# Reordering the units, the work ahead of the first unit and the slot fill in a mixture-of-experts layer whose weights stream from memory

## Chip, cores and metric

One core of one Trainium2 chip runs the whole program. The metric is device time in microseconds (us) of one execution, the median over several. The chip's parts are named as in the profile: PE is TensorE, DVE is VectorE, ACT is ScalarE, POOL is GpSimd, SP is SyncE, which here only issues transfers.

## The reference, cut to what matters

Two trunk layers over 384 tokens (128 context, 256 latent) of width 1024. In each layer a mixer (convolution, Hyena and attention groups) is followed by a mixture of 64 experts, of which each token takes 8, and by one shared expert that takes all tokens. Only the mixture is touched:

```python
def swiglu(x, wg, wu, wd):
    return (jax.nn.silu(x @ wg) * (x @ wu)) @ wd

def moe(h, p):
    s = jax.nn.sigmoid(h @ p['router_w'])
    # 4 of 8 groups by their two best (s + bias), then the 8 best experts in them
    w = w / jnp.sum(w, axis=-1, keepdims=True) * ROUTED_SCALE
    # every expert runs on the tokens that chose it; results are weighted and summed per token
    y_buf = lax.map(expert_block, (x_buf, block_e))
    routed = jax.ops.segment_sum(y_buf * w_buf[:, None], tok_buf, ...)
    return swiglu(h, p['sh_w_gate'], p['sh_w_up'], p['sh_w_down']) + routed
```

An expert has three fp32 matrices, gate and up (1024 x 256 each) and down (256 x 1024): 1 MiB each, 3 MiB an expert, 192 MiB for the 64 experts of a layer. All are read in each layer.

## The kernel before, in words

**Units.** The experts are sorted by their number of tokens and get fixed numbers of slots: 11 experts of 96 slots are paired with 11 of 32, 38 of 64 slots are paired among themselves, and 4 get 128 slots alone. So there are 34 units of 128 slots: 30 pair units (numbers 0 to 29; 0 to 10 are 96 and 32) and 4 full units (30 to 33). `parts` gives a unit's slots, `WIDE` the order in which the units run, `JOBS` the experts n = 1 to 64 in that order, `OWNER` the step that uses n. Before, the order begins with the full units 30 and 31, then pairs 0 to 5, full unit 32, pairs 11 to 17, full unit 33, and the other pairs.

**Buffers and SP.** Four weight buffers of 3 MiB (two in RING, two in WB) take the experts in turn: expert n goes to buffer n % 4. The shared expert is n = 0 and lies in buffer 0, which is next wanted by expert 4. SP issues the loads in program order from one queue (L517 and L518 the gate and up matrices, L522 the down matrix): for each step first gate and up of its experts, then their down matrices. `free` makes gate and up of n wait until the gate and up product of the step that owns n - 4 is done, and the down matrix until that step's down products are done; for n = 4 it waits for `sh_gu` and `sh_dn`, the last use of the shared expert's matrices for the third token tile. The stream starts when DVE has the order of the experts (`d_ord`, L1726). In layer 0 SP also loads the next layer's parameters after step 2.

**Ahead of the first unit, on PE (`mixture_pe`).** An order written out by hand mixes the routing's products (counts, order, positions: L1063 to L1086) with the shared expert's work for token tiles 1 and 2: `shared_up` (gate and up, 8 slices of k), `shared_flip` (transposes of the activation, L966), `shared_down` (two halves of columns, L959), two calls of `gate_rows` (L824, which lay the layer's output gate out as rows for ACT's `grow`), and `lists` for units 0 to 2 (L977, L980: which token sits in which slot). `lists` and `shared_flip` share PSUM bank 7.

**On DVE (`mixture_dve`).** After the positions are in place (`place`, from L1731), `onehot` builds a unit's slot matrix (L1766), `list_out` copies the list out of PSUM (L1776), `lst` turns it into gather indices (L1784: 16 small operations, four for each quarter g of the slots) and weights, `shared` makes the shared activation, and `turned` transposes the gathered rows of a unit (L1831).

**On POOL (`mixture_pool`).** `gather` issues four indirect DMAs a unit (L564). Issue g fetches the rows of slots 32g to 32g + 31, each in four parts of 1 KB: partition 32r + i takes part r of the row of slot 32g + i. Indices of empty slots are out of bounds, and their rows aren't moved. A unit's filled slots are, in each expert's range, the first ones. `scat` builds the matrix that sends a unit's outputs back to tokens (L572).

**A step (`step`, on PE).** Gate and up products of the unit (L946, 8 slices of k, both experts of a pair in parallel column groups), lists of unit s + 3, scatter of unit s - 1 (L993, L994), transposes (L966), down products (L959). Step 0 has the second half of the shared down product of tile 2 in place of the scatter.

## Time and profile before

| | |
|---|---|
| median of 3 runs | 1730.71 us (1730.41 to 1733.8) |
| the profiled execution | 1731.37 us, span 1729.5 us |
| PE busy | 1583.1 us (92%) |
| DVE, ACT, POOL busy | 840.1, 346.4, 425.5 us |
| DMA | 530.59 MB, mean 307 GB/s |
| experts' loads, first layer | first issued at 315.3 us of the span |
| experts' loads, second layer | first issued at 1163.6 us |

A window's row gives, behind the window and its length, the busy time of PE, of its weight loads (PEld), DVE, ACT and POOL with the number of instructions in brackets, then the granted TensorE clock (1.00 is 2.4 GHz, 0.50 is 1.2 GHz), the mean busy share of the 16 DMA engines (it shows 1.01 to 1.02 where all are busy) and the GB/s moved. A timeline row gives the start, the duration, engine, line, operation, output and inputs, and in square brackets the idle time before it with what ended it. Matmuls overlap, so a group of PE rows lasts a few tenths less than shown where another follows at once.

### The profile page before, as it was taken

Reading aid. Unit: us, or ns where it says so; the run is one execution under the profiler, and the core shown is the slowest. Engines: PE = TensorE matmul, PEld = TensorE weight load, DVE = VectorE, ACT = ScalarE, POOL = GpSimd, SP = SyncE. Lnnn points to the kernel's source line nnn. Section 1 sums busy time; section 2 is a strip of 40 time slices with the busy share of each in tenths; the row PEclk is TensorE's granted clock in tenths of the full one; section 3 lists DMA queues with packets and bytes.
Section 4 is the critical chain, followed back from the end, with each engine's and each line's share of the span. In section 5 each row is a group of like instructions: output and inputs, shape, how many; then the busy total and the mean of one; then the engine's idle time right before and its main releaser. Section 6 shows DMA issues by size and latency. Waiting matters only on the chain.

```text
span 1729.5 us, 22727 instructions
## 1 busy us (share of the span) xinstructions
PE 1583.1 (92%) x7900; PEld 791.3 (46%) x7900; DVE 840.1 (49%) x2813; ACT 346.4 (20%) x776; POOL 425.5 (25%) x421
## 2 busy tenths in 40 slices
PE   6999899899998998888979997998999899889886
PEld 2865355544443434434347553554444344344333
DVE  3777553644443443444165856455444434343332
ACT  2501443111111111111152014431111111111111
POOL 0300010143332332333013000004333323332320
PEclk9999999999999999999989999999999999999998
DMA  9322825779999999999632239028999999999993
GB/s 398 142 104 98 345 105 195 292 290 413 413 413 413 413 412 412 413 413 414 285 128 98 104 104 395 1 82 333 369 412 412 416 413 412 412 414 413 413 415 141
DMA packets 80851, 530.59 MB, mean 307 GB/s; under 512 B 13968, under 2 KB 17308, under 8 KB 25184
## 3 DMA queue, kind: packets, MB, share of 16 engines
q1 hardware_dynamic: 67680, 503.90, 71.9%
q0 software_dynamic: 13056, 25.22, 4.0%
q8 instruction: 64, 1.05, 0.2%
q14 instruction: 51, 0.42, 0.1%
HBM read 533.76 MB, written 5.77 MB: 312 GB/s over the span
## 4 chain that ended last, share of the span: by engine, by line
PE 58%; DMA 31%; DVE 6%; issue 2%; SPq 2%; ACT 1%; POOL 0%; DVEq 0%; ACTq 0%
PE PSB L946 21%; DMA WB<-in_exp_w_up 21%; DMA RING<-in_exp_w_up 8%; PE PSB L938 7%; PE PSB L959 6%; PE PSB L874 4%; PE PSB L993 2%; PE PSB L994 2%; PE PSB L689 2%; PE PSB L910 1%; PE PSB L920 1%; PE PSB L911 1%; PE PSB L933 1%; SPq L517 1%; PE PSB L732 1%
## 5 line engine op out<-in xcount | busy, mean ns | idle before, releaser
L946 PE MATMUL PSB<-RING,EX 128*32 128x512 f32 (+2 forms) x1344 | 409.1, 608 | 44.9 <-DMA WB<-in_exp_w_up 31.1
L946 PE MATMUL PSB<-WB,EX 128*32 128x512 f32 (+2 forms) x1408 | 417.8, 600 | 30.1 <-DMA RING<-in_exp_w_up 23.3
L564 POOL DMA_INDIRECT XG<-h_rows,IDX x272 | 279.0, 1026 | 181.2 <-issue 94.4
L959 PE MATMUL PSB<-RING,AT 128*32 128x512 f32 (+2 forms) x720 | 227.0, 598 | 4.8 <-ACT GROW L1298 3.7
L572 POOL TENSOR_SCALAR SCAT<-CST,LSTT 128x384 fp32r<-128x384 f32 x68 | 84.9, 1248 | 561.3 <-PE PSB L994 561.1
L946 PEld LDWEIGHTS PSB<-WB,EX 128*32 128x32 f32 (+2 forms) x1408 | 128.2, 127 | 191.1 <-issue 191.1
L946 PEld LDWEIGHTS PSB<-RING,EX 128*32 128x32 f32 (+2 forms) x1344 | 123.2, 128 | 199.0 <-issue 199.0
L959 PE MATMUL PSB<-WB,AT 128*32 128x512 f32 (+2 forms) x704 | 210.8, 596 | 0.0
L1852 DVE TENSOR_TENSOR YL<-PSB,YH 128x512 fp32r<-128x512 f32 x136 | 94.0, 691 | 186.0 <-ACT YH L1378 186.0
L1776 DVE COPY LCOL<-PSB 128x6 f32<-128x6 f32 x68 | 11.2, 164 | 345.8 <-PE PSB L977 312.8
L993 PE MATMUL PSB<-YH,SCAT 128*128 128x512 f32 x408 | 171.8, 421 | 2.8 <-DVE YL L1852 2.8
L1784 DVE TENSOR_SCALAR IDX<-LCOL 32x1 int32<-32x1 f32 x1088 | 157.3, 145 | 31.9
L994 PE MATMUL PSB<-YL,SCAT 128*128 128x512 f32 x408 | 161.0, 395 | 0.0
L1371 ACT ACTIVATE SGM<-PSB 128x256 f32<-128x256 f32 x68 | 26.1, 383 | 531.6 <-PE PSB L946 531.6
L1378 ACT ACTIVATE YH<-PSB 128x512 fp32r<-128x512 f32 x136 | 81.2, 597 | 239.6 <-PE PSB L959 239.6
L938 PE MATMUL PSB<-RING,HT 128*128 128x512 f32 x288 | 125.9, 592 | 0.0
L556 POOL TENSOR_TENSOR ST<-ST,HALF 128x1 f32<-128x1 f32 x48 | 28.6, 595 | 301.4 <-DVE ST L2150 133.8
L959 PEld LDWEIGHTS PSB<-RING,AT 128*32 128x32 f32 (+2 forms) x720 | 62.8, 129 | 79.1 <-issue 75.2
L959 PEld LDWEIGHTS PSB<-WB,AT 128*32 128x32 f32 (+2 forms) x704 | 58.4, 126 | 72.4 <-issue 71.9
L993 PEld LDWEIGHTS PSB<-YH,SCAT 128*128 128x128 f32 x408 | 77.6, 190 | 21.2 <-issue 4.9
L1831 DVE STREAM_TRANSPOSE EX<-XG 128x1024 f32<-128x1024 f32 x68 | 84.2, 1238 | 6.4 <-DMA XG<-h_rows,IDX 6.3
L874 PE MATMUL PSB<-RING,YT 128*128 128x512 f32 x192 | 85.7, 593 | 0.0
(287 smaller groups left out, 1832.5 us busy)
## 6 DMA issues: line engine op xcount, KB each, us to landing
RING<-in_exp_w_gate SPq DMA_DIRECT2D x64, 1024.0 KB
RING<-in_exp_w_up SPq DMA_DIRECT2D x64, 1024.0 KB
RING<-in_exp_w_down SPq DMA_DIRECT2D x64, 1024.0 KB, 20.6
WB<-in_exp_w_gate SPq DMA_DIRECT2D x64, 1024.0 KB, 16.6
WB<-in_exp_w_up SPq DMA_DIRECT2D x64, 1024.0 KB, 20.6
WB<-in_exp_w_down SPq DMA_DIRECT2D x64, 1024.0 KB, 20.7
RING<-in_wmod SPq DMA_DIRECT2D x16, 2048.0 KB, 11.2
KSYS<-in_wmod SPq DMA_DIRECT2D x8, 2048.0 KB, 10.5
```

Source lines behind the costliest of these rows:

```text
L564: pool.indirect_dma_start(XG[:, s % 2, g * 256:(g + 1) * 256], None, h_quarters, bass.IndirectOffsetOnAxis(ap=IDX[:, s, g:g + 1], axis=0), ...
L572: nc.gpsimd.tensor_scalar(SCAT[:, s % 2, :], cst("iota"), LSTT[:, s:s + 1], None, ALU.is_equal).then_inc(p_scat, 1)
L874: mm = nc.tensor.matmul(PS[YB[0][t] + hf][:, :], YT[:, f, t * P:(t + 1) * P], w[:, f, :], start=(f == 0), stop=(f == 7))
L938: mm = nc.tensor.matmul(PS[3 + i % 3][:, :], HT[:, k, t * P:(t + 1) * P], w[:, k, :], start=(k == 0), stop=(k == KD - 1))
L946: mm = nc.tensor.matmul(PS[6][s0:s0 + w, :].rearrange("p (w f) -> p w f", w=2), e(k, s0, w), rawgu[n % NBUF][:, k], start=(k == 0), stop=( ...
L959: mm = nc.tensor.matmul(dst[s0:s0 + w, :], AT[:, j, s0:s0 + w], rawdn[n % NBUF][:, hf, j], start=(j == 0), stop=(j == 1))
L993: nc.tensor.matmul(PS[piece][:, :], w, YHb[s % 2][:, cols], start=False, stop=False, skip_group_check=True)
L994: mm = nc.tensor.matmul(PS[piece][:, :], w, YLb[s % 2][:, cols], start=False, stop=True, skip_group_check=True)
L1378: sc.activation(YHb[s % 2][:, hf * 512:(hf + 1) * 512], PS[6 + hf][:, :], ACT.Copy).then_inc(a_yh, 1)
L1784: v.tensor_scalar(IDX[32 * r:32 * r + 32, s, g:g + 1], LCOL[32 * g:32 * g + 32, 4:5], 4.0, 4.0 * NONE + r, ALU.mult, ALU.add).then_inc(d_l ...
L1831: v.transpose(EX2[:, s % 2].rearrange("p k (g j) -> p g k j", g=4), XG[:, s % 2, :].rearrange("p (g k j) -> p g k j", g=4, k=KD)).then_inc ...
L1852: v.tensor_tensor(YLb[s % 2][:, hf * 512:(hf + 1) * 512], PS[6 + hf][:, :], YHb[s % 2][:, hf * 512:(hf + 1) * 512].bitcast(F32), ALU.subtr ...
```

## The change

It has these parts:

- **Unit order.** `WIDE` begins with the pair units 0 to 5, 11, 12; the full units come at steps 8, 15, 22 and 29.
- **SP order.** The down matrix of expert 4 (now the second expert of step 1) is issued behind gate and up of step 2's experts.
- **PE order.** Both `gate_rows` move ahead of the position products, the shared gate and up slices move behind them, `lists` of unit 0 comes ahead of the last slices, and `lists` of unit 2 and the shared down products of tiles 1 and 2 move into step 0. Tile 2 has its own buffer AT2 for the transposed activation. ACT's and DVE's orders follow.
- **Gather waits.** Each of a unit's four gathers waits for its own four indices, not for the whole list.
- **DVE order.** The transpose of unit 0's rows comes ahead of unit 1's index operations, and that of unit 1 at the end of step 0's activation.
- **Slot fill.** In steps s >= 3 with s odd the slot matrix compares with reversed ranks (IOTAR), so that the filled slots are the last ones of each expert's range. IOTAR costs one DVE operation a layer.

```diff
@@ -162,7 +162,9 @@
             YL1 = sb("YL1", [P, DM], F32R, c=me)
-            sb("unused1", [P, (NT - 2) * DM], c=me)
+            AT2 = sb("AT2", [P, 2, P], c=me)
+            IOTAR = sb("IOTAR", [P, P], c=me)
+            sb("unused1", [P, (NT - 2) * DM - 3 * P], c=me)
@@ -272,7 +274,8 @@
-        WIDE = (30, 31) + tuple(range(0, 6)) + (32,) + tuple(range(11, 18)) + (33,) + tuple(range(6, 11)) + tuple(range(18, 30))
+        WIDE = (tuple(range(0, 6)) + (11, 12, 30) + tuple(range(13, 18)) + (6, 31) + tuple(range(7, 11)) + (18, 19, 32)
+                + tuple(range(20, 26)) + (33,) + tuple(range(26, 30)))
@@ -509,6 +512,7 @@
                 sp.wait_ge(d_ord, l + 1)
+                late = []
                 for s, job in enumerate(JOBS):
@@ -516,10 +520,15 @@
-                    for (n, c, cap, tiles), e in zip(job, es):
+                    for (n, c, cap, tiles), e in late + list(zip(job, es)):
                         b = n % NBUF
+                        if n == NBUF and s == OWNER[n]:
+                            late = [((n, c, cap, tiles), e)]
+                            continue
                         free(l, n, True)
                         sp.dma_start(raw[b][:, 4096:6144], row(I["exp_w_down"], l, e)).then_inc(dn_in[b], 16)
+                    if s > OWNER[NBUF]:
+                        late = []
@@ -557,16 +566,17 @@
             def gather(l, s):
-                pool.wait_ge(d_lst, LSTN * (NU * l + s + 1))
                 if s >= 2:
                     pool.wait_ge(d_ex, NU * l + s - 1)
                 for g in range(4):
+                    pool.wait_ge(d_lst, LSTN * (NU * l + s) + 4 * (g + 1))
                     pool.indirect_dma_start(XG[:, s % 2, g * 256:(g + 1) * 256], None, h_quarters,
...
             def scat(l, s):
+                pool.wait_ge(d_lst, LSTN * (NU * l + s + 1))
                 if s >= 2:
@@ -821,7 +831,7 @@
-                    mm = nc.tensor.matmul(PS[(2, 4)[r] + k // 4][:, (k % 4) * P:(k % 4 + 1) * P],
+                    mm = nc.tensor.matmul(PS[2 + k // 4][:, (k % 4) * P:(k % 4 + 1) * P],
@@ -951,12 +961,12 @@
-            def down(job, hf, dst):
+            def down(job, hf, dst, a=AT):
...
@@ -1006,14 +1016,22 @@
                 for k in range(KD):
                     mm = gate_up(job, slots(s % 2), k)
+                    if s == 0 and k == 3:
+                        pe.wait_ge(sh_ah, NT * l + 3)
+                        lists(l, 2)
                 mm.then_inc(pe_gu, 1)
                 if s > 0:
                     pe.wait_ge(d_yl, 2 * (NU * l + s))
+                else:
+                    pe.wait_ge(d_lcol, NU * l + 3)
                 if s + 3 < NU:
                     lists(l, s + 3)
                 if s > 0:
                     scatter(l, s - 1, (0, 1, 2, 3))
                 else:
+                    shared_down(l, 1, 0)
+                    shared_down(l, 1, 1)
+                    shared_down(l, 2, 0)
                     shared_down(l, 2, 1)
@@ -1046,10 +1064,10 @@
-                if t == 2 and hf == 0:
+                if t == 1 and hf == 0:
                     pe.wait_ge(a_grow, 8 * (l + 1))
                 pe.wait_ge(sh_ah, NT * l + t + 1)
-                mm = down(SHARED, hf, PS[2 * t + hf])
+                mm = down(SHARED, hf, PS[2 * t + hf], AT2 if t == 2 else AT)
@@ -1057,7 +1075,7 @@
                 shared_flip(l, 0)
-                shared_up(l, 1, 0, 3)
+                gate_rows(l, 1, 0)
                 pe.wait_ge(d_cnt, l + 1)
@@ -1074,36 +1092,31 @@
                 mm.then_inc(pe_ord, 1)
-                shared_up(l, 1, 3, 6)
+                shared_up(l, 1, 0, 2)
                 pe.wait_ge(d_sw, l + 1)
...
-                shared_up(l, 1, 6)
+                gate_rows(l, 1, 1)
                 pe.wait_ge(a_stk, l + 1)
...
                 mm.then_inc(pe_perm, 1)
+                shared_up(l, 1, 2, 6)
+                pe.wait_ge(sh_ah, NT * l + 1)
+                lists(l, 0)
+                shared_up(l, 1, 6)
                 shared_down(l, 0, 0)
                 shared_down(l, 0, 1)
-                lists(l, 0)
                 pe.wait_ge(d_lcol, NU * l + 1)
                 shared_flip(l, 1)
-                shared_up(l, 2)
-                pe.wait_ge(d_sort, SORTN * (l + 1))
-                gate_rows(l, 1, 0)
-                shared_down(l, 1, 0)
-                shared_down(l, 1, 1)
-                pe.wait_ge(d_lcol, NU * l + 1)
+                shared_up(l, 2, 0, 3)
+                pe.wait_ge(sh_ah, NT * l + 2)
                 lists(l, 1)
+                shared_up(l, 2, 3)
                 pe.wait_ge(d_lcol, NU * l + 2)
                 shared_flip(l, 2)
-                gate_rows(l, 1, 1)
-                pe.wait_ge(sh_ah, NT * l + 3)
-                lists(l, 2)
-                shared_down(l, 2, 0)
-                pe.wait_ge(d_lcol, NU * l + 3)
                 for s in range(NU):
@@ -1353,19 +1366,22 @@
             def mixture_act(l):
                 shared_turned(l, 0)
-                shared_sig(l, 1)
+                grow(l, 1, 0)
                 act.wait_ge(pe_sw, l + 1)
                 sc.activation(STK[:, :, :].rearrange("p t s -> p (t s)"), PS[5][:, 0:NT * P], ACT.Copy).then_inc(a_stk, 1)
+                grow(l, 1, 1)
+                shared_sig(l, 1)
                 shared_turned(l, 1)
                 shared_sig(l, 2)
-                grow(l, 1, 0)
                 shared_turned(l, 2)
-                grow(l, 1, 1)
@@ -1763,7 +1779,8 @@
-                    ins = v.tensor_tensor(ONEHOT[:, s % 2, :, s0:s0 + cap], cst("iota")[:, 0:cap].unsqueeze(1).to_broadcast([P, NT, cap]),
+                    ranks = IOTAR[:, P - cap:P] if s >= 3 and s % 2 == 1 else cst("iota")[:, 0:cap]
+                    ins = v.tensor_tensor(ONEHOT[:, s % 2, :, s0:s0 + cap], ranks.unsqueeze(1).to_broadcast([P, NT, cap]),
@@ -1812,16 +1829,14 @@
                 onehot(l, 0)
-                shared(l, 1)
+                onehot(l, 1)
                 list_out(l, 0)
                 lst(l, 0)
-                onehot(l, 1)
-                shared(l, 2)
-                onehot(l, 2)
+                shared(l, 1)
                 list_out(l, 1)
-                lst(l, 1)
-                list_out(l, 2)
-                lst(l, 2)
+
+                dve.wait_ge(h_out, 16 * NT * (l + 1))
+                do(v.tensor_scalar(IOTAR[:, :], cst("iota")[:, 0:P], -1.0, float(P - 1), ALU.mult, ALU.add), d_rt)
@@ -1832,10 +1847,15 @@
                 turned(0)
+                lst(l, 1)
+                shared(l, 2)
+                onehot(l, 2)
+                list_out(l, 2)
+                lst(l, 2)
                 for s in range(NU):
                     if s + 3 < NU:
                         onehot(l, s + 3)
-                    if s + 1 < NU:
+                    if 1 <= s < NU - 1:
                         turned(s + 1)
@@ -1847,6 +1867,8 @@
                     if s + 3 < NU:
                         lst(l, s + 3)
+                    if s == 0:
+                        turned(1)
```

## Rows read from the trace of the kernel before

**Rows 1.** Profile page: the gathers' DMA queue (packets, MB, share) and the chain by engine.
```profile
q0 software_dynamic: 13056, 25.22, 4.0%
...
PE 58%; DMA 31%; DVE 6%; issue 2%; SPq 2%; ACT 1%; POOL 0%; DVEq 0%; ACTq 0%
```

**Rows 2.** Windows: start:end, length, busy by engine, granted clock, DMA share, GB/s.
```profile
318.00:344.00 26.00, 22.71 (x89) 12.83 (x87) 13.71 (x78) 5.94 (x9) 6.62 (x7) 0.97 1.01 419
344.00:384.00 40.00, 38.73 (x153) 18.08 (x152) 19.62 (x74) 4.31 (x9) 17.74 (x17) 0.93 0.73 278
384.00:840.00 456.00, 418.97 (x2356) 186.78 (x2357) 193.74 (x774) 58.44 (x119) 156.37 (x146) 0.99 1.01 413
1194.00:1232.00 38.00, 37.44 (x163) 17.91 (x165) 19.42 (x81) 4.69 (x10) 16.89 (x17) 1.00 0.71 267
```

**Rows 3.** Chain that ended last, end of the first layer's loads: start, us, what.
```profile
814.32 24.39 DMA WB<-in_exp_w_up
838.80 9.83 PE PSB L946 x32
```

**Rows 4.** The same chain, a pair unit and full unit 32: start, us, what.
```profile
445.91 7.07 PE PSB L946 x64
...
460.11 7.07 PE PSB L946 x16
```

**Rows 5.** Timeline of the SP queue, first layer: start, us, instruction.
```profile
315.29 0.37 SPq L517 DMA_DIRECT2D RING<-in_exp_w_gate  x1
...
331.75 0.34 SPq L517 DMA_DIRECT2D RING<-in_exp_w_gate  x1
...
356.49 0.33 SPq L522 DMA_DIRECT2D RING<-in_exp_w_down  x1
```

**Rows 6.** Timeline of PE, first layer, 313 to 355.
```profile
313.60 2.79 PE L946 MATMUL PSB<-RING,HT 128*128 128x512 f32 x6
...
319.29 0.94 PE L1086 MATMUL PSB<-PERM,STK 128*128 128x128 f32 x6 [0.85 <-ACT STK L1363]
320.06 3.60 PE L959 MATMUL PSB<-RING,AT 128*128 128x512 f32 x8
...
324.52 7.03 PE L946 MATMUL PSB<-RING,HT 128*128 128x512 f32 x16
331.39 1.95 PE L824 MATMUL PSB<-CST,GC 128*128 128x128 f32 x16
...
345.21 9.20 PE L946 MATMUL PSB<-RING,EX 128*128 128x512 f32 x16 [0.71 <-DVE EX L1831]
```

**Rows 7.** Timeline of PE, second layer, the same gate and up product.
```profile
1193.59 7.11 PE L946 MATMUL PSB<-RING,EX 128*128 128x512 f32 x16 [1.59 <-DVE EX L1831]
```

**Rows 8.** Timeline of DVE, first layer.
```profile
322.71 0.56 DVE L1766 TENSOR_TENSOR ONEHOT<-CST,POSS 128x384 fp32r<-128x384 f32 x1
...
324.16 2.78 DVE L1784 TENSOR_SCALAR IDX<-LCOL 32x1 int32<-32x1 f32 x16
...
343.82 1.25 DVE L1831 STREAM_TRANSPOSE EX<-XG 128x1024 f32<-128x1024 f32 x1
```

**Rows 9.** Timeline of POOL, first layer.
```profile
328.20 1.27 POOL L564 DMA_INDIRECT XG<-h_rows,IDX  x1 [30.81 <-DVE LSTW L1790]
...
332.38 1.00 POOL L564 DMA_INDIRECT XG<-h_rows,IDX  x1 [0.30 <-issue]
```

**Rows 10.** Tile XG, 400 to 840: time of the gathers from issue to landing.
```profile
DMA to landing us min/median/max: 5.8/6.3/7.8
```

**Rows 11.** Windows at the end of each layer's loads: columns as in Rows 2.
```profile
845.00:858.00 13.00, 13.00 (x62) 5.75 (x60) 2.29 (x4) 1.96 (x4) 1.24 (x1) 1.00 0.47 196
1690.00:1703.00 13.00, 13.00 (x62) 5.71 (x60) 2.29 (x4) 1.96 (x4) 1.24 (x1) 1.00 0.54 226
```

**Rows 12.** Short windows inside the first of these.
```profile
846.00:848.00 2.00, 2.00 (x12) 0.65 (x10) 0.00 (x0) 0.00 (x0) 0.00 (x0) 1.00 0.83 340
...
854.00:856.00 2.00, 2.00 (x12) 0.66 (x10) 0.69 (x1) 0.88 (x2) 0.00 (x0) 1.00 0.24 98
```

More of the change, by code:

```diff
@@ L958, in down @@
                         for s0, w in tiles:
-                            mm = nc.tensor.matmul(dst[s0:s0 + w, :], AT[:, j, s0:s0 + w], rawdn[n % NBUF][:, hf, j],
+                            mm = nc.tensor.matmul(dst[s0:s0 + w, :], a[:, j, s0:s0 + w], rawdn[n % NBUF][:, hf, j],
                                                   start=(j == 0), stop=(j == 1))
@@ L1298, in grow @@
                     own.sig(sc.activation(g[:, cond, 4 * b:4 * b + 4, :],
-                                          PS[(2, 4)[r] + b][:, :].rearrange("t (k q) -> t k q", k=4), ACT.Copy), a_grow)
+                                          PS[2 + b][:, :].rearrange("t (k q) -> t k q", k=4), ACT.Copy), a_grow)
             def squares(l, r, t):
@@ L1355, in shared_turned @@
                 act.wait_ge(sh_at, NT * l + t + 1)
-                sc.activation(AT[:, :, :].rearrange("p j s -> p (j s)"), PS[7][:, 0:DE], ACT.Copy).then_inc(sh_ah, 1)
+                if t == 2:
+                    act.wait_ge(h_out, 16 * NT * (l + 1))
+                a = AT2 if t == 2 else AT
+                sc.activation(a[:, :, :].rearrange("p j s -> p (j s)"), PS[7][:, 0:DE], ACT.Copy).then_inc(sh_ah, 1)
             def mixture_act(l):
                 shared_turned(l, 0)
-                shared_sig(l, 1)
+                grow(l, 1, 0)
                 act.wait_ge(pe_sw, l + 1)
                 sc.activation(STK[:, :, :].rearrange("p t s -> p (t s)"), PS[5][:, 0:NT * P], ACT.Copy).then_inc(a_stk, 1)
+                grow(l, 1, 1)
+                shared_sig(l, 1)
                 shared_turned(l, 1)
                 shared_sig(l, 2)
-                grow(l, 1, 0)
                 shared_turned(l, 2)
-                grow(l, 1, 1)
                 for s in range(NU):
```

## The prediction

> **What bounds the kernel now.** I read the page first: PE is busy 92% of the span, yet the chain that ended last has 31% DMA in it [rows 1]. The windows say where. From 384 to 840, nearly the whole first mixture, all 16 DMA engines are busy (share 1.01 at 413 GB/s), and PE is busy 419 of 456 us [rows 2]; just before, from 344 to 384, the share is 0.73, and in the second layer 0.71 for 38 us, with PE at work nearly throughout. So a layer's mixture is a stream of weights that nothing in it shortens, with a hole of 40 x (1 - 0.73/1.01) = 11.1 us near its start in the first layer and 38 x (1 - 0.71/1.01) = 11.3 us in the second. At the other end the chain goes from a load that lands at 838.7 straight to the product that waited for it [rows 3], and from there PE alone sets the end: whatever makes the stream's last loads land earlier shortens the layer one for one. Faster PE work inside the stream is worth nothing.
>
> **Why there is a hole.** The chain shows a pair unit's gate and up products taking 7.07 us, and those of full unit 32 also 7.07 us [rows 4]: a pair's experts run side by side. Between these two starts lie 14.2 us, a whole step. A pair brings 6 MiB in that time, which at 413 GB/s is 15.2 us of stream; a full unit brings 3 MiB, 7.6 us. With full units first, PE spends two steps on freeing what feeds the stream for 15 us. In the SP queue [rows 5] the loads start at 315.29, expert 4's gate matrix is issued at 331.75 and its down matrix only at 356.49, after the shared expert's last down product; SP issues in order, so everything else stands behind it. By then 11 MiB and two units' gathers are issued: a unit's gathers are 25.22 MB / 68 = 0.37 MB [rows 1]. That is 12.3 MB, or 29.3 us at the 419 GB/s of this stretch [rows 2], and the stream runs dry at 345.6.
>
> **The change at the start, step by step (first layer).** The start of the stream is fixed by the expert order, whose products end ahead of 313.60 [rows 6]; ahead of them two gate_rows (the first only) replace three slices, and a row of gate_rows (1.95) is shorter than what it replaces, 3/8 of 7.03 [rows 6]. I cost that at nothing. From 313.60: two slices 1.75 (2/8 of 7.03), three transposes of SW (0.4, by half of the six in L1086's 0.94), the second gate_rows 1.8 as it overlaps, so the position products start at 317.5 where they started at 319.29 [rows 6]: they no longer wait for ACT's STK, which stood behind a sigmoid. DVE's slot matrix follows 3.4 us behind, at 320.9 and not 322.71; those of units 0 and 1 end at 322.2, as one for a pair costs about what the full one's 0.56 does [rows 8]. PE's four slices last until 321.9, the list until 322.5; DVE's 16 index operations (2.78) begin at 322.7, and the first four are done at 323.4 [rows 8]. Before, POOL's first gather began at 328.20, 1.0 after the whole list was done; now it waits for four indices, begins at 324.4, and the fourth, 4.2 us behind the first as before, at 328.6 instead of 332.38 [rows 9]. The median from issue to landing is 6.3 [rows 10], so unit 0's rows are there at 334.9, and the transpose (1.25, [rows 8]) ends at 336.1. Before, the transpose waited until 343.82 behind DVE's index work.
>
> DVE has a new order, and that is where the change waits: the transpose stands ahead of unit 1's indices (2.78, and 0.3 for its three small operations), and the shared activation of tile 2 (two operations a little smaller than a slot matrix's 0.56, 0.9) behind them. It ends at 340.1. PE, with 1.75 + 3.6 + 0.4 + 2.65 + 0.7 + 4.4 = 13.5 us of slices, down products and list behind 322.5, is through at 336.0 and idles 4 us. Then a transpose of 0.4, and the first product starts at 340.5 and not 345.21. With unit 2's list in its middle it takes 7.1 + 0.5, to 348.1. The 0.4, 0.5 and 0.7 are estimates from 0.94 for six small products [rows 6].
>
> SP: expert 4's gate can go when tile 2's slices end, at 336.0 and not 331.75. The stream has 8 MiB and one unit's gathers, 8.8 MB or 20.9 us from about 316.3, until 337.2; with the 1.3 that I take from issue to data it just meets it. No row isolates that time: its bounds are 0 and the fastest gather's 5.8 [rows 10], and I stay near the lower, since SP's loads need no indices fetched; each layer's hole moves one for one with it, before as after, so it cancels in the difference but for this meeting. Its down matrix no longer blocks: it goes behind experts 5 and 6, whose gates wait only for step 0's product at 348.1. Hence the hole runs from 345.6 to 349.4, **3.8 us**. Next are 4 MiB (10.2 us), to 359.6; expert 4's down matrix is free after four shared down halves of 1.8 [rows 6], 348.7 + 7.1 = 355.8, in time. Step 0's down products end at 360.8 and free 2 MiB; step 1 then frees gate buffers at 367.9, when the stream has work to 367.7 (in the first layer the parameters' 1 MiB more). I allow 0.2 in the first layer and 1.2 in the second. Holes of 4.0 and 5.0 stand against 11.1 and 11.3: **gain 7.1 + 6.3 = 13.4 us**. POOL's gathers for unit 1 end issuing near 341.7 and land near 348, its transpose is wanted only at 360.8; the matrices of `scat` keep their place. In later steps a full unit takes PE 14 us against 8.5 of stream, a deficit of 5.5, a pair 14 against 16.1: six pairs between two full units bring 12 and cover it. I cost the four late full units at nothing; without the cover each costs up to 5.5 us.
>
> **Slot fill.** At the ends of the streams the busy share doesn't fall at once: 845 to 858 it is 0.47, 1690 to 1703 it is 0.54 [rows 11]. Against the mean engine, the last one ends (1 - 0.47/1.01) x 13 = 7.0 us late in the first layer and 6.1 in the second. The weights are equal rows for all; the gathers move 0.37 MB where full slots would be 0.52 (4 x 128 x 1 KB), and the empty ones are always each range's last. Bounds: 0, if an engine's share doesn't hang on the slot, and 7.0 + 6.1. The fall is gradual (0.83 at 846, 0.24 at 854, [rows 12]), as a sloping share of gather work over the engines would give, so I take the upper end less a tenth for steps 0 to 2, filled forward, and chance: **gain 6.3 + 5.4 = 11.7 us**. The Trainium skill's DMA: Bandwidth & Descriptors, The descriptor swizzle, gives the engine of a 128-partition transfer by its group of four partitions, modulo eight within each half; with this gather's index layout that is the slot's group of four modulo eight, which reversed ranks mirror. By it the gain would be near 12. No row here names an engine.
>
> **Sum.** 1731.4 - 13.4 - 11.7 = 1706.3 for the profiled execution, which lies 0.7 above the median: **1706** rounded. The reversed-ranks operation, less than a slot matrix's 0.56, is hidden in DVE's wait for rows.
>
> **Rivals.**
> - *The slope isn't from the slots.* Then 13.4 alone: 1718. For it: no row shows which engine carries what. Against it: the gradual fall. Chance 0.15. The skill's same page, Latency and other measured facts, says engines 7 and 15 are usually slower; two late engines of 16 would leave a share near 0.12 throughout, and the levels of 0.83 and 0.24 here speak against that rule.
> - *The first product gains nothing*, since PE's 4 us idle brings the clock to 1.2 GHz or DVE is later. Half clock cost 9.20 against 7.11 [rows 6, 7], 2.1 a layer; the whole loss is 13.4: 1719. Chance 0.12.
> - *It doesn't do what it says*: neither hole nor slope moves, 1730. Chance 0.04.
> - *Slower: unit 0's rows come late.* DVE's transpose now blocks unit 1's indices and tile 2's activation, and PE and SP stand behind that. Each us of later landing makes the hole a us longer. It takes 14 us a layer, 20 from issue to landing instead of 6.3, to be slower by 0.2%; at 22, 1706 + 2 x 16 = 1738. The slowest gather took 7.8 [rows 10]. Chance 0.03.
> - *More is gained*: no hole at all, 9.0, 1697. Chance 0.08.
>
> **The numbers.** The forecast has 0.58. The range takes in the two part-gains above and most of the best case: 1698 to 1719. Apart by 0.2% (3.5 us) is about what a measurement of this kernel can tell. Faster: 0.58 + 0.15 + 0.12 + 0.08 = 0.93; same 0.04; slower 0.03.
>
> **What would show it.** In the new profile: position products at 317.5, first gather 324.4, first unit's product at 340.5; expert 4's down matrix issued behind those of experts 5 and 6's gates; a hole of about 4 us from 345.6; the share at the stream's end falling from 1.0 to 0 within 3 us; full units' steps with PE waiting no less in the pairs around them. A hole of 10 us, a tail as long as before, or DMA share under 1.0 around steps 15, 22 and 29 would prove me wrong.

## The result, and the profile after

The changed kernel takes **1715.26 us** (median of 4 executions, 1713.72 to 1716.95) where the kernel before takes 1731.14 beside it (1730.41 to 1733.8): a ratio of 0.9896 with a 95% interval of 0.9879 to 0.9914, some 16 to 18 us less. Run again later it took 1715.84, ratio 0.9897 (0.9879 to 0.9915). So it is faster, within the range of 1698 to 1719, but 9 us above the 1706 of the forecast: of 25.1 us expected, about two thirds came. Two executions of this study, one of the kernel before (2312.13 us, mean granted clock 0.657) and one of a variant below (2709.96 us, 0.556), ran at a far lower clock than the 0.97 to 0.98 of all others and are left out of the ratios.

The page of the changed kernel: the first rows and the chain by engine, which answer to [rows 1].

```profile
span 1714.6 us, 22803 instructions
...
PE 1583.5 (92%) x7900; PEld 792.1 (46%) x7900; DVE 841.0 (49%) x2815; ACT 347.2 (20%) x776; POOL 426.2 (25%) x421
...
DMA packets 80852, 530.60 MB, mean 309 GB/s; under 512 B 13968, under 2 KB 17308, under 8 KB 25184
...
PE 62%; DMA 26%; DVE 6%; issue 2%; ACT 1%; SPq 1%; POOL 0%; DVEq 0%; ACTq 0%
```

Work and bytes are the same as before (the gathers' queue too, 25.22 MB); what changed is waiting. The chain has 26% DMA in it and not 31%.

Windows of the same kernel: the start of each layer's stream, its middle and its end, to be laid beside [rows 2, 11].

```profile
344.00:384.00 40.00, 38.68 (x282) 15.11 (x285) 19.67 (x84) 4.31 (x9) 17.39 (x17) 0.97 0.93 371
384.00:840.00 456.00, 429.74 (x2280) 194.02 (x2273) 195.95 (x780) 59.31 (x121) 156.85 (x146) 0.99 1.02 413
838.00:851.00 13.00, 12.03 (x56) 5.34 (x54) 2.29 (x4) 1.96 (x4) 1.24 (x1) 1.00 0.58 241
847.00:849.00 2.00, 2.00 (x12) 0.86 (x10) 0.01 (x1) 0.00 (x0) 0.00 (x0) 1.00 0.12 49
1188.00:1226.00 38.00, 36.75 (x269) 14.45 (x265) 19.59 (x84) 3.93 (x8) 14.87 (x14) 0.98 0.84 336
1676.00:1689.00 13.00, 12.05 (x56) 5.37 (x54) 2.29 (x4) 1.97 (x4) 1.24 (x1) 1.00 0.64 267
1686.00:1688.00 2.00, 2.00 (x12) 0.86 (x10) 0.00 (x0) 0.00 (x0) 0.00 (x0) 1.00 0.07 29
```

Read with the prediction's method. The holes are (1 - 0.93/1.02) x 40 = 3.5 us and (1 - 0.84/1.02) x 38 = 6.7 us; before they were 11.1 and 11.3. (Run again, the changed kernel had shares of 0.93 and 0.90 in the same windows: 3.5 and 4.5 us.) The middle is saturated as before, at the same 413 GB/s, with all four full units in it, so the late full units cost nothing. At the ends, whose windows here stop with the last load (851.0 and 1689.1), the mean engine is (1 - 0.58/1.02) x 13 = 5.6 and (1 - 0.64/1.02) x 13 = 4.8 us ahead of the last; before it was 7.0 and 6.1. So the start gave 7.6 + 4.6 = 12.2 us, nearly the 13.4 forecast, and the ends 1.4 + 1.3 = 2.7 where 11.7 was forecast. Together that is 14.9 of the 16 to 18 us measured.

The chain at the end of the first layer's loads, which answers to [rows 3] (start, us, what):

```profile
825.68 20.84 DMA RING<-in_exp_w_up
...
846.61 7.09 PE PSB L956 x32
```

Still a load that lands last and a product that waited for it, now for the last unit. Before, the load at 838.7 was that of the last unit but one. PE then worked without a wait, and the chain of the kernel before has the last unit's product as

```profile
855.44 6.88 PE PSB L946 x32
```

with nothing of DMA ahead of it. So before, the chain left the DMA engines 6 us ahead of the window in which the busy share falls (845 to 858), and what lands last, the down matrices at 858.0, wasn't wanted until 865.5. The prediction had counted the whole lateness in that window as time of the layer. Nor is the product behind the wait the same: it took 9.83 us, with the granted clock at 0.55 from 838 to 845, and takes 7.09 in the changed kernel.

Timelines of the changed kernel around the first unit, first layer: SP, POOL, DVE, PE. A row has start, us, engine, line, operation, output and inputs, and the idle time before it.

```profile
318.79 0.37 SPq L521 DMA_DIRECT2D RING<-in_exp_w_gate  x1
...
352.98 0.34 SPq L521 DMA_DIRECT2D RING<-in_exp_w_gate  x1
...
361.00 4.79 SPq L529 DMA_DIRECT2D RING<-in_exp_w_down  x2
...
326.82 1.27 POOL L573 DMA_INDIRECT XG<-h_rows,IDX  x1 [26.47 <-DVE IDX L1801]
...
331.01 1.00 POOL L573 DMA_INDIRECT XG<-h_rows,IDX  x1 [0.30 <-issue]
...
338.06 1.25 DVE L1846 STREAM_TRANSPOSE EX<-XG 128x1024 f32<-128x1024 f32 x1 [4.53 <-DMA XG<-h_rows,IDX]
339.23 2.75 DVE L1801 TENSOR_SCALAR IDX<-LCOL 32x1 int32<-32x1 f32 x16
...
342.89 0.42 DVE L1815 TENSOR_TENSOR ACTV<-PSB,ACTV 128x256 f32<-128x256 f32 x1
...
320.42 0.83 PE L1104 MATMUL PSB<-PERM,STK 128*128 128x128 f32 x6
...
333.06 4.54 PE L956 MATMUL PSB<-RING,HT 128*128 128x512 f32 x10
343.46 0.67 PE L976 MATMUL PSB<-CST,ACTV 128*128 128x128 f32 x2 [5.86 <-DVE ACTV L1815]
344.06 1.08 PE L956 MATMUL PSB<-RING,EX 128*32 128x512 f32 x3
```

DVE stands idle for 4.53 us waiting for unit 0's rows, then does the transpose, unit 1's indices and tile 2's activation one after the other, and PE waits 5.86 us for the last of them. That is the wait the prediction named, only longer.

### The profile page after: what moved, and what is told of

It is laid out like the page before. It is cut to its first block, busy times and chain, and to the rows that moved or that the text cites. A ratio compares the mean times of both kernels' runs of the same rounds, so it can differ in the third digit from the quotient of the medians.

```text
span 1714.6 us, 22803 instructions
## 1 busy us (share of the span) xinstructions
PE 1583.5 (92%) x7900; PEld 792.1 (46%) x7900; DVE 841.0 (49%) x2815; ACT 347.2 (20%) x776; POOL 426.2 (25%) x421
## 3 DMA queue, kind: packets, MB, share of 16 engines
q0 software_dynamic: 13056, 25.22, 4.0%
## 4 chain that ended last, share of the span: by engine, by line
PE 62%; DMA 26%; DVE 6%; issue 2%; ACT 1%; SPq 1%; POOL 0%; DVEq 0%; ACTq 0%
PE PSB L956 22%; DMA RING<-in_exp_w_up 16%; DMA WB<-in_exp_w_up 8%; PE PSB L969 7%; PE PSB L948 7%; PE PSB L884 4%; PE PSB L1003 3%; PE PSB L1004 3%; PE PSB L699 2%; PE PSB L943 1%; PE PSB L920 1%; PE PSB L930 1%; PE PSB L921 1%; PE PSB L742 1%; SPq L521 1%
## 5 line engine op out<-in xcount | busy, mean ns | idle before, releaser
L956 PE MATMUL PSB<-RING,EX 128*32 128x512 f32 (+2 forms) x1408 | 375.1, 610 | 28.7 <-DMA RING<-in_exp_w_up 14.8
L956 PE MATMUL PSB<-WB,EX 128*32 128x512 f32 (+2 forms) x1344 | 373.3, 600 | 23.9 <-DMA WB<-in_exp_w_up 12.9
L969 PE MATMUL PSB<-RING,AT 128*32 128x512 f32 (+2 forms) x752 | 210.5, 596 | 1.1 <-ACT AT L1389 1.1
L956 PEld LDWEIGHTS PSB<-RING,EX 128*32 128x32 f32 (+2 forms) x1408 | 115.8, 127 | 185.8 <-issue 185.8
L956 PEld LDWEIGHTS PSB<-WB,EX 128*32 128x32 f32 (+2 forms) x1344 | 115.8, 127 | 177.4 <-issue 177.4
L969 PE MATMUL PSB<-WB,AT 128*32 128x512 f32 (+2 forms) x672 | 189.1, 597 | 0.0
L969 PEld LDWEIGHTS PSB<-WB,AT 128*32 128x32 f32 (+2 forms) x672 | 51.9, 126 | 69.3 <-issue 68.9
## 6 DMA issues: line engine op xcount, KB each, us to landing
RING<-in_wmod SPq DMA_DIRECT2D x16, 2048.0 KB, 11.3
```

Source lines behind the costliest of these rows:

```text
L956: mm = nc.tensor.matmul(PS[6][s0:s0 + w, :].rearrange("p (w f) -> p w f", w=2), e(k, s0, w), rawgu[n % NBUF][:, k], start=(k == 0), stop=( ...
L969: mm = nc.tensor.matmul(dst[s0:s0 + w, :], a[:, j, s0:s0 + w], rawdn[n % NBUF][:, hf, j], start=(j == 0), stop=(j == 1))
```

## The experiments

All are edits of the kernel before, of the changed one, or of the version with indices first below; each shows the lines that matter. The text on record stands ahead of each measurement. Times are medians; "before" is the kernel before on the same chip, 1732.44 for the first four, 1733.75 for the next four and 1732.55 for the last four. The holes and latenesses are worked out from windows as above, by 1.01 or 1.02 as the middle of the stream shows it.

### The slot fill: four runs

**Fill alone.** The kernel before, with reversed ranks in odd steps from step 3 on, and nothing else:

```diff
+            IOTAR = sb("IOTAR", [P, P], c=me)
...
+                    ranks = IOTAR[:, P - cap:P] if s >= 3 and s % 2 == 1 else cst("iota")[:, 0:cap]
...
```

> The kernel before with the reversed fill in odd steps from 3 on and nothing else. In the trace of the changed kernel the last DMA engine ends 10.9 us (first layer) and 7.9 us (second) sooner after the first load than before, of which the shorter hole explains 8.0 and 4.9. Theory: the rest, 3.0 us a layer, is the slot fill's, so this kernel takes 1731 - 6 = 1725 us, and its busy share at the streams' ends falls within about 6 us instead of 12. As forecast (11.7 us for the fill): 1719 us. Rival (the fill does nothing, the rest has another cause): 1731 us and a fall over 12 us.

Measured: 1729.8 us (10 executions, 1726.45 to 1732.74), ratio 0.9985 (0.9971 to 1.0): 2.6 us, at most 5. The 11.7 of the forecast is far outside, and so is the theory's 6. Its windows at the ends of the streams and around the second layer's hole, and that last one for the kernel before:

```profile
843.00:856.00 13.00, 12.01 (x55) 5.45 (x55) 2.29 (x4) 1.97 (x4) 1.24 (x1) 1.00 0.67 279
1689.00:1702.00 13.00, 12.00 (x56) 5.43 (x54) 2.29 (x4) 1.97 (x4) 1.24 (x1) 1.00 0.72 297
1188.00:1232.00 44.00, 41.33 (x157) 19.23 (x158) 23.02 (x97) 5.55 (x12) 20.16 (x19) 0.92 0.68 262
```
```profile
1188.00:1232.00 44.00, 39.99 (x169) 18.95 (x172) 24.61 (x109) 6.65 (x12) 20.55 (x20) 1.00 0.75 287
```

The lateness falls from 7.0 and 6.1 to (1 - 0.67/1.01) x 13 = 4.4 and (1 - 0.72/1.01) x 13 = 3.7 us, 5.0 less in all and not 11.7: even with balanced slots more than half of it stays. And not all of the 5.0 shows in the time. In this profile the second layer's hole is (1 - 0.68/1.01) x 44 = 14.4 us where it was 11.3, with its first product at the lower clock (9.07 us and not the 7.11 of [rows 7]). Whether other executions lost time in the same way isn't known.

**Everything but the fill**, and **all units from the last slot on.** The changed kernel with one condition altered:

```diff
-                    ranks = IOTAR[:, P - cap:P] if s >= 3 and s % 2 == 1 else cst("iota")[:, 0:cap]
+                    ranks = IOTAR[:, P - cap:P] if False else cst("iota")[:, 0:cap]
```

> The changed kernel with every unit filled forward. Theory (the fill is worth 3.0 us a layer): 1715 + 6 = 1721 us, the share at the end falls over 12 us again, the holes near the start stay at about 3 and 6 us. As forecast (11.7): 1727 us. Rival (the fill does nothing): 1715 us.

```diff
+                    ranks = IOTAR[:, P - cap:P] if s >= 3 else cst("iota")[:, 0:cap]
```

> The changed kernel with all steps from 3 on filled from the last slot. If an engine's gather work hangs on the slot alone and the engines are otherwise equal, this is the mirror image of the forward fill: same time as that kernel, 1721 us by the theory, and a fall over 12 us. In the changed kernel one of 16 engines still ends 3 us behind the others in both layers (a share of 0.06 for 3 us). If it is one of those that the first slots load, the mirror image takes work from it: the share of 0.06 at the end goes, and the time is 1718 us. If it is one that the last slots load, its lateness adds to the load: 1724 us or more. Rival (the fill does nothing): 1715 us.

Measured: forward 1718.8 (1717.03 to 1722.01), ratio 0.9919 (0.9903 to 0.9936); all reversed 1719.41 (1716.81 to 1720.65), ratio 0.9923 (0.9906 to 0.994). Against 0.9896 of the alternating fill both are 4 to 5 us slower, and equal to each other; their intervals overlap that of the changed kernel at the edge.

The same windows at the ends of the streams, each stopping within 0.7 us of its last load: forward, then all reversed.

```profile
843.00:856.00 13.00, 12.05 (x56) 5.44 (x54) 2.29 (x4) 1.96 (x4) 1.24 (x1) 1.00 0.54 224
1682.00:1695.00 13.00, 12.03 (x56) 5.43 (x54) 2.29 (x4) 1.96 (x4) 1.24 (x1) 1.00 0.61 254
```
```profile
841.00:854.00 13.00, 12.07 (x56) 5.61 (x56) 2.29 (x4) 1.96 (x4) 1.24 (x1) 1.00 0.57 235
1680.00:1693.00 13.00, 12.06 (x56) 5.61 (x56) 2.29 (x4) 1.96 (x4) 1.24 (x1) 1.00 0.63 260
```

The shares hardly differ from the 0.58 and 0.64 of the changed kernel: here too most of the lateness at a stream's end is there with balanced slots. What follows: the slots do matter, since only the mixture of both directions gains and one direction is worth what the other is. But the fill is worth about 4 us in both layers together, and the fall at the end is a poor measure of it. On the kernel before it fell by 5.0 us for 2.6 of time; between these profiles it differs by 1 us at most for 4 of time, and forward fill under the changed start already ends a little less late (6.1 and 5.2) than before (7.0 and 6.1).

A fourth run settles the size on another base (the version with indices first, below), where no hole interferes:

```diff
-                    ranks = IOTAR[:, P - cap:P] if s >= 3 and s % 2 == 1 else cst("iota")[:, 0:cap]
+                    ranks = IOTAR[:, P - cap:P] if False else cst("iota")[:, 0:cap]
```

> The kernel with the index operations first and every unit filled forward. The fill was worth 0.23% of the time, some 4 us, on the changed kernel, and 0.15% on the kernel before. Theory (it works in the stream, whatever the start does): 4 to 5 us more than the kernel beside it, 1710 us, and the busy share at the stream's end falls over 9 us or more. Rival (part of it was given back in the holes): 7 us or more.

Measured: 1710.06 (1707.81 to 1711.28), ratio 0.9867 (0.9845 to 0.9889), against 1705.53, ratio 0.9843 (0.982 to 0.9866), of its base in the same session: 4.2 us by the ratios, 4.5 by the medians. That is the theory's 4 to 5, and not the rival's 7. The intervals overlap, but four comparisons by ratios (2.6 for the fill alone, 4.0 and 4.7 against forward and all reversed, 4.2 here) say the same.

### The DVE order ahead of the first unit

```diff
-                turned(0)
                 lst(l, 1)
                 shared(l, 2)
+                turned(0)
                 onehot(l, 2)
```

> The changed kernel with DVE's index operations of unit 1 and the shared activation of tile 2 ahead of the transpose of unit 0's rows. In the changed kernel DVE idles 4.5 us before that transpose and PE 5.9 us behind the work that comes after it. Theory (the hole that is left hangs on this order): the first unit's product starts 3.7 us sooner, the first layer's hole of 3 us goes, the second layer's of 6.4 us shrinks to about 3, and the time falls by 6 to 7 us to 1708 or 1709. Rival (what holds the stream is expert 4's gate, issued when tile 2's slices end): product sooner, hole and time as they are, 1715 us.

Measured: **1705.29** (1703.54 to 1710.61), ratio 0.9854 (0.9831 to 0.9877): 7 to 10 us faster than the changed kernel. Its timeline of PE and of SP, and two windows, one in each layer:

```profile
330.07 4.54 PE L956 MATMUL PSB<-RING,HT 128*128 128x512 f32 x10
336.09 0.48 PE L976 MATMUL PSB<-CST,ACTV 128*128 128x128 f32 x2 [1.49 <-DVE ACTV L1815]
337.24 0.63 PE L956 MATMUL PSB<-RING,EX 128*32 128x512 f32 x3 [0.67 <-DVE EX L1846]
...
345.09 0.34 SPq L521 DMA_DIRECT2D RING<-in_exp_w_gate  x1
...
344.00:384.00 40.00, 38.76 (x283) 16.73 (x275) 20.97 (x91) 4.92 (x11) 16.38 (x16) 1.00 1.02 412
...
1182.00:1222.00 40.00, 39.43 (x287) 16.97 (x290) 20.39 (x85) 5.20 (x11) 16.02 (x15) 1.00 1.01 404
```

DVE now does the index work and the activation while the rows are on their way, instead of behind them. PE waits 1.49 us and not 5.86, in this profile its clock is 1.00 throughout, and the next gates are issued 29.3 us after the first load (315.80), while by the prediction's account the stream has work until 30.3 after: the shares are 1.02 and 1.01, both holes are gone. The wait of 5.86 us was worth the whole remaining hole, and more than the 6 to 7 us expected. So the prediction's small rival "more is gained" was there to be had, one swap away.

The same kernel again, as the base for later runs:

> The changed kernel with unit 1's index operations and tile 2's activation ahead of unit 0's transpose, again, beside the kernels of this call. Ratio to the kernel before 0.985 as in the first call, 1705 to 1708 us, no hole in either layer.

Measured: 1705.53 (1702.53 to 1707.72), ratio 0.9843 (0.982 to 0.9866). PE waits the same 1.49 us in its profile, but here the clock does fall, to 0.74 from 338 to 342 and 0.84 from 342 to 346. The stream has no hole all the same (shares of 1.01 from 344 to 384 and 1.02 from 1174 to 1214).

### The parts of the start: order, down matrix, gather waits

**The changed kernel with the old unit order:**

```diff
+        WIDE = (30, 31) + tuple(range(0, 6)) + (32,) + tuple(range(11, 18)) + (33,) + tuple(range(6, 11)) + tuple(range(18, 30))
```

> The changed kernel with the unit order of the kernel before (full units 30 and 31 first), all else as changed. Theory (a full unit takes PE the 14 us of a step and frees only 3 MiB of the stream): holes of 11 us or more in each layer, in two or three pieces, and 1731 us, as before the change. Rival (the moved shared down products and the earlier gathers carry the gain, the order of the units nothing): 1715 us, holes of 3 and 6 us.

Measured: 1734.11 (10 executions, 1730.41 to 1736.13), ratio 0.9997 (0.9985 to 1.0009). Its SP timeline and its windows, one in each layer:

```profile
354.51 0.34 SPq L520 DMA_DIRECT2D RING<-in_exp_w_gate  x1
...
374.08 0.33 SPq L520 DMA_DIRECT2D WB<-in_exp_w_gate  x1
...
350.00:380.00 30.00, 28.65 (x82) 14.26 (x81) 17.02 (x80) 3.32 (x7) 11.83 (x11) 1.00 0.58 216
1198.00:1224.00 26.00, 24.72 (x69) 11.90 (x68) 14.15 (x62) 2.34 (x5) 9.49 (x9) 0.99 0.38 135
```

A full unit's product frees one expert's gate and up, and between two such releases (354.51 and 374.08) lies more than a step. The holes are (1 - 0.58/1.01) x 30 = 12.8 and (1 - 0.38/1.01) x 26 = 16.2 us. All other parts of the change together show no gain without the order.

**The kernel before with the new unit order alone:**

```diff
+        WIDE = (tuple(range(0, 6)) + (11, 12, 30) + tuple(range(13, 18)) + (6, 31) + tuple(range(7, 11)) + (18, 19, 32)
+                + tuple(range(20, 26)) + (33,) + tuple(range(26, 30)))
```

> The kernel before with the new unit order and nothing else. Theory (SP issues in order, and expert 4's down matrix waits for tile 2's down product at the end of step 0): one hole of about 10 us stays in each layer, the short ones behind it go, 1728 to 1730 us. Rival (the order alone carries the gain of the start): holes of 3 and 6 us, 1718 us.

Measured: 1726.71 (10 executions, 1724.73 to 1729.91), ratio 0.9973 (0.996 to 0.9986): 4.7 us by the ratio, 7.0 by the medians. The windows around its two holes:

```profile
350.00:361.00 11.00, 10.44 (x85) 4.10 (x81) 4.79 (x23) 0.77 (x2) 6.72 (x7) 1.00 0.38 120
1194.00:1205.00 11.00, 10.44 (x81) 3.75 (x85) 4.52 (x21) 0.77 (x2) 7.29 (x7) 0.99 0.40 113
```

Holes of 6.9 and 6.6 us are left of 11.1 and 11.3, 8.9 less, and 5 to 7 us of it show in the time. In the profiled executions the two mixtures, each from its first load to the last activation, take 11.6 us less than before, while the whole takes 5.3 less (1726.04 against 1731.37). The rest lies outside the mixtures: the first load comes at 319.83 and not 315.29, and 1.7 us more lie between the first mixture and the second.

**The changed kernel with expert 4's down matrix issued in its old place:**

```diff
-                        if n == NBUF and s == OWNER[n]:
+                        if False:
```

> The changed kernel with expert 4's down matrix issued in its own step, ahead of gate and up of experts 5 and 6. It waits for tile 2's down product, which now comes behind step 0's gate and up product. Theory (SP issues in order): gates 5 and 6 are issued 8 to 9 us later, each hole grows by as much, 1715 + 17 = 1732 us, as much as the whole change had gained. Rival (the stream has enough issued by then): 1715 us.

Measured: 1727.63 (median of 10; nine of them from 1725.8 to 1730.08), ratio 0.9971 (0.9957 to 0.9986): 12 to 13 us slower than the changed kernel where 17 was expected. Its SP timeline and two windows:

```profile
361.69 0.33 SPq L529 DMA_DIRECT2D RING<-in_exp_w_down  x1
363.35 0.34 SPq L521 DMA_DIRECT2D RING<-in_exp_w_gate  x1
...
344.00:384.00 40.00, 38.53 (x275) 15.24 (x279) 20.23 (x87) 4.31 (x9) 18.03 (x17) 0.96 0.75 289
1190.00:1230.00 40.00, 38.75 (x279) 15.04 (x273) 19.58 (x84) 3.92 (x8) 15.69 (x15) 0.96 0.74 286
```

SP stands at the down matrix until 361.69, and the gates of experts 5 and 6, which could go at 352.98 in the changed kernel, go at 363.35. The holes are back at 10.6 and 11.0 us. That is 42.4 us after this execution's first load (319.27), as before it was 41.2 [rows 5]: without the deferral the queue stands at the same place as ever, and 5 us by the ratio are left of the gain, as with the new unit order alone.

**The changed kernel with each gather waiting for the whole list again:**

```diff
-                    pool.wait_ge(d_lst, LSTN * (NU * l + s) + 4 * (g + 1))
+                    pool.wait_ge(d_lst, LSTN * (NU * l + s + 1))
```

> The changed kernel with each gather waiting for its unit's whole list again. Theory (unit 0's rows are what DVE's order waits for): its first gather starts 2.5 us later after the first load, the first product as much later, each hole is 2.5 us longer, 1715 + 5 = 1720 us. Rival (the hole hangs on tile 2's slices or on SP): product later, time as it is, 1715 us.

Measured: 1718.99 (1717.76 to 1720.12), ratio 0.992 (0.9903 to 0.9937): 3 to 4 us slower. Its POOL and PE timelines:

```profile
328.43 1.27 POOL L573 DMA_INDIRECT XG<-h_rows,IDX  x1 [30.71 <-DVE LSTW L1807]
...
344.63 0.67 PE L976 MATMUL PSB<-CST,ACTV 128*128 128x128 f32 x2 [7.96 <-DVE ACTV L1815]
```

The first gather goes later behind its list, and PE's wait grows from 5.86 to 7.96 us. The windows from 348 to 358 and from 1189 to 1198 (shares 0.32 and 0.36) hold 6.9 and 5.8 us of hole, 12.7 together. The changed kernel had 10.2 in its first profile and 8.0 in its second, so that is 2.5 to 4.7 more, around what the time shows.

### The changed kernel again, and one step further

> The changed kernel again, beside the kernels of this call. Ratio to the kernel before 0.990, 1714 to 1717 us; holes of 3 us (first layer) and 6 us (second). The second layer's larger hole goes with a first product at the 1.2 GHz clock; theory: where the clock stays at 2.4 GHz the hole is 2 us smaller.

Measured: 1715.84 (1714.06 to 1716.71), ratio 0.9897 (0.9879 to 0.9915). Its profile shows the same wait of PE, 5.99 us, and holes of 3.5 and 4.5 us. The theory that goes with them isn't borne out: the second layer's hole is 2.2 us smaller than in the first profile, although the clock was just as low (0.50 from 1184 to 1188, 0.82 from 1188 to 1192).

**Indices first, and the next layer's parameters loaded behind the experts.** Once the stream has no hole, every byte in it is on the path; the 1 MiB of parameters isn't wanted until the next layer.

```diff
-                    if s == 2 and l + 1 < DEPTH:
-                        sp.dma_start(PR[:, :], I["par"][l + 1]).then_inc(par_in, 16)
+                if l + 1 < DEPTH:
+                    sp.dma_start(PR[:, :], I["par"][l + 1]).then_inc(par_in, 16)
                 sp.wait_ge(pe_dn, 2 * NU * (l + 1))
```

> The kernel with the index operations first, and the next layer's parameters (1 MiB) loaded behind the last expert's matrices instead of behind step 2's. With no hole left the stream's bytes set the first layer. Theory: 1.05 MB at 413 GB/s are 2.5 us that move from the stream into PE's last 14 us, where no DMA runs: 2.5 us less than the kernel beside it, 1703 us, and the first layer's last expert load ends 2.5 us sooner after the first. Rival (the stream isn't the bound any more, PE is): no change.

Measured: **1703.31** (1700.92 to 1707.08), ratio 0.9838 (0.9816 to 0.9861), against 0.9843 of its base in the same session. 2.2 us by the medians, and not told apart by the intervals. The traces point the same way: by their chains the first layer's last matrices that PE waits for land 520.7 us after the first load (817.87 + 20.84 - 318.02) where they land 523.9 after it in the base (821.65 + 20.84 - 318.59), 3.2 sooner for 2.5 expected. It is the fastest version of the study, 28 to 29 us ahead of the kernel before.

## Why the prediction was right, and where it was wrong

**The bound and the hole: right.** The step times forecast for the first layer, as us after the first load (forecast from 315.29; the load came at 318.79 in the profiled execution):

| step | forecast | measured |
|---|---|---|
| position products start | 2.2 | 1.6 |
| first, fourth gather | 9.1, 13.3 | 8.0, 12.2 |
| transpose of unit 0's rows starts | 19.6 | 19.3 |
| PE through with its work | 20.7 | 18.8 |
| PE idle | 4 | 5.86 |
| first product starts | 25.2 | 25.3 |
| next gates issued | 32.8 | 34.2 |
| hole, first and second layer | 4.0, 5.0 | 3.5, 6.7 |

The first product came within 0.1 us, partly by luck: by the chain unit 0's last gather took 6.96 from issue to landing, not 6.3, and it was issued 1.1 earlier. Expert 4's down matrix was issued 42.2 after the first load and not the 40.5 forecast; it was in time even so. The next gates were issued 1.4 us later than forecast and the hole is 0.5 smaller all the same: the stream held out some 2 us longer than the 30.3 of the sum, which counts 1.0 us from the first issue to its data and 1.3 from the next gates' issue to theirs. Full units cost nothing, as forecast. So the first term, 13.4 us, measured 12.

**The rival "the first product gains nothing" was partly true.** PE's idle time was followed by a lower clock. Windows of the changed kernel around the first product, first layer and second (the third number from the end is the granted clock):

```profile
344.00:348.00 4.00, 4.00 (x29) 1.08 (x32) 0.00 (x0) 0.38 (x1) 2.51 (x3) 0.71 1.03 408
348.00:352.00 4.00, 4.00 (x39) 1.35 (x35) 2.29 (x16) 0.00 (x0) 0.67 (x1) 1.00 0.63 250
...
1184.00:1188.00 4.00, 4.00 (x22) 1.06 (x25) 0.24 (x2) 0.38 (x1) 2.85 (x3) 0.50 1.03 411
1188.00:1192.00 4.00, 4.00 (x35) 1.17 (x31) 0.88 (x6) 0.00 (x0) 0.00 (x0) 0.83 0.24 90
1192.00:1196.00 4.00, 3.32 (x28) 1.15 (x21) 2.92 (x18) 0.38 (x1) 2.74 (x3) 1.00 0.16 45
```

In the second layer PE runs at 1.2 GHz (0.50) after an idle of 5.78 us, until about 1189, and the product that was to take 7.6 us lasts from 1184.41 to past 1194. In the first layer the clock was low for less time. The price was 2.1 a layer in the rival; on the product it came out near 1 and 2.5, less than would have been needed to undo the whole first term. It isn't all of what makes the second layer's hole 6.7 us and not 5.0. Run again, the product was as slow (1184.02 to past 1194) and the hole 4.5, because the product began 24.8 us after that layer's first load (1159.18) and not 27.1 (1157.29).

**The failed step is in "Slot fill": "I take the upper end less a tenth".** The bounds of this term were 0 and 13.1 us, and nothing in the trace said which part of the lateness was slope from the slots. The gradual fall of the share was taken as its sign, but a gradual fall is there with the balanced fill too: of 13.1 us of lateness the fill alone took 5.0. And the upper bound took all lateness for time of the layer, while the chain of the kernel before leaves the DMA engines at 838.7, ahead of that fall. How much each of the two accounts for isn't told apart. Measured, the term is worth 4 us, not 11.7: the missing 8 us are nearly the whole miss of 9. The rival "the slope isn't from the slots" (1718, 0.15) was closer in time than the forecast, though not true either: the slots give a third of what was forecast. The Trainium skill's DMA: Bandwidth & Descriptors, The descriptor swizzle, gives the engine by the group of four partitions, from which the prediction worked out a gain near 12. The runs agree with it in kind (forward and reversed alike, mixed better) and not with that size, and the measurement decides. With two ends so far apart and no row between them, the middle would have been the better value, and 1711 the forecast (1731.4 - 13.4 - 6.6). That the range held is owed to the first term and to its width: it took in a fill worth nothing.

**What is left at the end of the streams is open.** In the changed kernel the share is 0.12 from 847 to 849, 0.06 from 849 to 851 and 0.07 from 1686 to 1688: on average two engines of 16, and then one (1/16 is 0.06), are still moving weights when the others are done. One such engine was there before too (0.06 from 856 to 858). The Trainium skill's DMA: Bandwidth & Descriptors, Latency and other measured facts, says that engines 7 and 15 are usually slower, which the prediction set aside because the levels before were higher; such a level is what it would leave once the slope is gone. No row names the engine. The run with all units reversed was a partial test: an engine that is late and gets the rows of the last slots should have brought it to 1724 us or more, and it took 1719.41, about what the forward one took (1718.8). So nothing shows a slow engine among those, and what makes the last engine late stays open.

**Parts don't add.** The order alone gives 5 to 7 us, all the rest without it 0, and both 16 to 18. Each part only takes off what ends the hole last: with full units first, it is the rate at which buffers come free; with pairs first, SP's queue behind expert 4's down matrix; with that deferred, PE's wait for the activation; with that gone, the stream.

**Between two profiled executions, some us are chance.** From 210 to 250, attention that the change doesn't touch, the granted clock is 0.87 in the changed kernel and 0.96 before, and the expert loads start 3.5 us later. The profile of the kernel before is the shortest of all outside the mixtures: its first load comes at 315.29, in the 13 others at 315.8 to 322.1, and from the first mixture's last activation to the second's first load it takes 294.4 us, the others 295.7 to 298.0. The rows, of the changed kernel and then of the one before:

```profile
210.00:250.00 40.00, 35.81 (x166) 19.99 (x159) 27.02 (x89) 16.49 (x55) 3.86 (x7) 0.87 0.43 181
```
```profile
210.00:250.00 40.00, 35.63 (x176) 19.35 (x168) 27.05 (x89) 17.78 (x57) 3.84 (x7) 0.96 0.43 180
```

So the terms were compared from each layer's first load on, and not by the span.

## What to carry to other kernels

When a stream of loads is the bound, draw up for its first 50 us what each release frees and what stands behind it in the issuing queue: here the order of the units and one deferred transfer decided it, and either alone gave little. On an engine that waits for a transfer, put the work that others wait for ahead of the wait: one swap on DVE was worth half as much as the whole change. Where a term's bounds are nothing and the whole of what one sees, run the one-line experiment first or take the middle, and ask whether what one sees lies on the chain that sets the end.

## What the runs showed that was not expected

- Idles of 5.2 to 6.0 us of PE were followed by a stretch at 1.2 GHz in both layers of both profiles of the changed kernel, so that a wait of DVE on rows cost twice. A wait of 1.49 us is no safe side: in the version with indices first the clock stayed at 1.00 in one profile and fell to 0.74 in the other.
- The lower clock also stood at the end of a layer. In the kernel before, PE waited 3.44 us for the matrices of the last unit but one, and then its clock was 0.55 from 838 to 845. The product took 9.83 us, 7.09 in the changed kernel. It lies on the chain, and the prediction has no term for it.
- With gathers filled from both ends in turn the 16 DMA engines still don't end together: the last is 4.8 to 5.6 us behind the mean after 532 us of saturated stream, about 1%.
